# Scale and shift in halves of the features, and four projection chunks summed side by side by row blocks

## The reference

```python
    c_act = jax.nn.silu(c)
    mod = (c_act @ w_ada[l] + b_ada[l])[:, None, :]
    shift1, scale1, gate1, shift2, scale2, gate2 = jnp.split(mod, N_MOD, axis=-1)
    h = _rmsnorm(x, g_mix[l]) * (1.0 + scale1) + shift1
    proj = h @ w_in[l]
    a_u, a_v, b_q, b_k, b_v, c_q, c_k, c_v = jnp.split(proj, splits, axis=-1)
    # y_a: spatial gating, y_b: stick-breaking attention, y_c: dilated window attention with rope
    y = jnp.concatenate([y_a, y_b, y_c], axis=-1) @ w_out[l]
    x = x + (1.0 + gate1) * y
    ...   # a gated feed-forward with a short convolution, then an attention layer and a gated
    ...   # linear attention layer, each with a feed-forward, and a last norm
```

## Time and profile before

| | us |
|---|---|
| median of 3 runs | 939.43 |
| lowest, highest | 937.7, 939.97 |
| the profiled execution, its time | 938.27 |
| its span, first to last instruction | 936.5 |
| PE busy | 912.4 (97%) |
| DVE busy | 612.8 (65%) |
| ACT busy | 497.3 (53%) |

### The profile page before, as it was taken

How to read it: one execution, slowest core, us unless ns; L and a number is a source line. 1 busy time by engine, 2 the same in 40 slices (tenths; PEclk the granted TensorE clock), 3 DMA queues, 4 the chain that set the end, 5 groups by cost and what they waited for, 6 DMA issues and landing times.

```text
span 936.5 us, 17379 instructions
## 1 busy us (share of the span) xinstructions
PE 912.4 (97%) x7209; PEld 844.4 (90%) x7209; DVE 612.8 (65%) x970; ACT 497.3 (53%) x729; POOL 0.2 (0%) x4
## 2 busy tenths in 40 slices
PE   5899999999999999999999999999999999999997
PEld 2688788999999999878999999998999999988886
DVE  0665685786776775887765555576886765566664
ACT  3537774754555567665634434346656653344333
POOL 0000000000000000000000000000000000000000
PEclk9899999999999999999999999999999999999999
DMA  9998757676555578414365565555442655555541
GB/s 350 346 315 276 269 181 250 210 253 208 170 175 215 180 172 179 99 48 151 121 210 192 193 198 194 187 180 180 124 148 94 222 176 172 191 181 181 180 135 45
DMA packets 130698, 176.85 MB, mean 189 GB/s; under 512 B 19696, under 2 KB 108188, under 8 KB 130620
## 3 DMA queue, kind: packets, MB, share of 16 engines
q1 hardware_dynamic: 129852, 173.58, 56.8%
q10 hardware_dynamic: 768, 2.16, 0.7%
HBM read 174.68 MB, written 1.05 MB: 188 GB/s over the span
## 4 chain that ended last, share of the span: by engine, by line
PE 86%; DVE 6%; ACT 4%; DMA 2%; issue 2%; SPq 0%; ACTq 0%; DVEq 0%
PE psum L1591 25%; PE psum L1583 22%; PE psum L1584 21%; PE psum L1587 4%; PE psum L1588 4%; DMA raw<-in_w_ada_dram 2%; DVE w_lo L956 2%; PE psum L1685 1%; ACT w_hi L526 1%; PE psum L2190 1%; PE psum L2124 1%; PE psum L2145 1%; PE psum L2134 1%; DMA raw<-in_w_in_dram 1%; DVE h_lo L994 1%
## 5 line engine op out<-in xcount | busy, mean ns | idle before, releaser
L526 ACT ACTIVATE w_hi<-raw 128x2048 fp32r<-128x2048 f32 (+1 forms) x139 | 264.4, 1904 | 150.0 <-PE psum L1591 122.1
L1583 PE MATMUL psum<-h_hi,w_hi 128*128 128x256 f32 x1352 | 329.0, 283 | 1.5 <-DVE h_lo L1128 1.1
L956 DVE TENSOR_TENSOR w_lo<-raw,w_hi 128x2048 fp32r<-128x2048 f32 (+1 forms) x139 | 313.1, 2277 | 24.5 <-ACT w_hi L526 24.5
L1584 PE MATMUL psum<-h_lo,w_hi 128*128 128x256 f32 x1352 | 324.9, 280 | 0.0
L1583 PEld LDWEIGHTS psum<-h_hi,w_hi 128*128 128x128 f32 x1352 | 254.4, 188 | 11.0 <-issue 7.9
L1584 PEld LDWEIGHTS psum<-h_lo,w_hi 128*128 128x128 f32 x1352 | 255.0, 189 | 0.8
L1591 PE MATMUL psum<-h_hi,w_lo 128*128 128x256 f32 x1352 | 187.0, 280 | 0.7 <-DVE w_lo L956 0.5
L1591 PEld LDWEIGHTS psum<-h_hi,w_lo 128*128 128x128 f32 x1352 | 170.2, 188 | 1.5 <-DVE w_lo L956 1.3
L1324 DVE SCALAR_TENSOR_TENSOR arena<-psum,rstd 128x256 f32<-128x256 f32 x64 | 26.9, 424 | 132.0 <-PE psum L1591 130.1
L1583 PE MATMUL psum<-a_hi,w_hi 128*128 128x256 f32 x464 | 110.7, 280 | 0.6 <-DVE a_lo L1311 0.4
L1584 PE MATMUL psum<-a_lo,w_hi 128*128 128x256 f32 x464 | 110.3, 279 | 0.0
(11 more groups left out here) (274 smaller groups left out, 911.2 us busy)
## 6 DMA issues: line engine op xcount, KB each, us to landing
raw<-in_mlp_w_in_dram SPq DMA_DIRECT2D x32, 1024.0 KB, 5.6
raw<-in_mlp_w_out_dram SPq DMA_DIRECT2D x32, 1024.0 KB, 7.2
raw<-in_w_ada_dram SPq DMA_DIRECT2D x24, 1024.0 KB, 7.5
raw<-in_w_up_dram SPq DMA_DIRECT2D x22, 1024.0 KB, 5.1
raw<-in_gla_w_in_dram SPq DMA_DIRECT2D x12, 1024.0 KB, 5.3
raw<-in_w_down_dram SPq DMA_DIRECT2D x11, 1024.0 KB, 5.5
raw<-in_w_in_dram SPq DMA_DIRECT2D x10, 1024.0 KB, 8.1
raw<-in_w_out_dram SPq DMA_DIRECT2D x4, 1024.0 KB, 6.0
```

Source lines behind the costliest of these rows:

```text
L526: act.activation(halved(w_hi, m % SPLIT_SLOTS, SPLITS[m]), halved(raw, r % RAW_SLOTS, SPLITS[m]), ACT.Copy).then_inc(*mark("w_hi", m))
L956: dve.tensor_tensor(halved(w_lo, m % SPLIT_SLOTS, key), halved(raw, r % RAW_SLOTS, key), halved(w_hi, m % SPLIT_SLOTS, key).bitcast(F32), ...
L1583: pe.matmul(dst, high, both[0], start=start, stop=False, skip_group_check=True)
L1584: return pe.matmul(dst, high, both[1], start=False, stop=False, skip_group_check=True)
```

## The change

Scale and shift are both loaded and summed in halves of the features: pieces (1, 0), (1, 1), (0, 0), (0, 1) give scale and shift of feature tiles 0 to 3, and then two **row blocks** of `w_in` follow; a row block (`rows_in`) is 256 rows of the first four chunks, 1 MB in two DMAs. Then come the same six loads for tiles 4 to 7. The four chunks are summed side by side, two tiles in each of the banks 0 to 3: `rows_high` makes a block's 32 products with `w_hi`, `rows_low` its 16 with `w_lo`. Each half of scale and shift has its own turn (four transposes of 128 x 128), reduction and bias. `x` is turned first, with two of its four copies on DVE. The sums are copied out after the fourth block (`evict`). No `w_ada` pieces stand beside the first four chunks any more; the chunks 4 to 8 have two each. The six ropes and `w_sp` all stand behind in 4, `win_a` 0 to 3 behind in 5, and the turning of `rows` 2 to 4 and mod 2 behind in 6. The loads of constants move with them.

```diff
-ADA_BESIDE = [0, 1, 1, 2, 1, 1, 1, 1, 2, 1, 1]
+ADA_BESIDE = {4: 2, 5: 2, 6: 2, 7: 2, 8: 2, 9: 1, 10: 1}
+FIRST_CHUNKS = 4
...
-    s = [("ada", p, q) for p in (1, 0) for q in range(4)]
-    s.insert(5, ("in", 0))
-    for n in range(11):
-        s += [("in", n)] if n > 0 else []
-        s += [ada.pop(0) for _ in range(ADA_BESIDE[n])]
+    s = []
+    for half in range(2):
+        s += [("ada", p, 2 * half + j) for p in (1, 0) for j in range(2)] + [("rows_in", 2 * half + j) for j in range(2)]
+    for n in range(FIRST_CHUNKS, 11):
+        s += [("in", n)] + [ada.pop(0) for _ in range(ADA_BESIDE[n])]
...
-    extra = {0: [("angles",)], 1: [("rope", 0), ("rope", 1)], 2: [("rope", 2), ("rope", 3)], 3: [("rope", 4), ("rope", 5), ("w_sp",)],
-             4: [("win_a", 0), ("win_a", 1), ("rows", 2), ("rows", 3), ("rows", 4)],
-             5: [("win_a", 2)],
-             6: [("win_a", 3), ("stick_a", 0), ("stick_a", 1)],
+         ("round", 0), ("first", 0), ("round_low", 0), ("rows_high", 0), ("part", 1, 2), ("round", 1), ("round_low", 1),
+         ("rows_low", 0, 0), ("rows_low", 0, 1), ("part", 1, 3), ("angles",), ("rows_high", 1),
+         ("mod", 1, 1), ("gains", 0, 1), ("normed", 0, 1), ("part", 0, 2), ("part", 0, 3), ("rows_low", 1, 0), ("mod", 0, 1),
+         ("rows_low", 1, 1), ("round", 2), ("first", 1), ("round_low", 2), ("rows_high", 2), ("round", 3), ("round_low", 3),
+         ("rows_low", 2, 0), ("rows_low", 2, 1), ("rows_high", 3), ("round", 4), ("rows_low", 3, 0), ("rows_low", 3, 1),
+         ("evict", 0), ("evict", 1), ("round_low", 4), ("evict", 2), ("evict", 3)]
+    extra = {4: [("rope", t) for t in range(6)] + [("w_sp",)],
+             5: [("win_a", 0), ("win_a", 1), ("win_a", 2), ("win_a", 3)],
+             6: [("rows", 2), ("rows", 3), ("rows", 4), ("mod", 2), ("stick_a", 0), ("stick_a", 1)],
...
+                if kind == "rows_in":
+                    w = a["w_in"][0]
+                    return [(0, row_chunk(w[:, IN_COLS[0]:IN_COLS[0] + 3 * S], n * S)),
+                            (3 * S, row_chunk(w[:, IN_COLS[3]:IN_COLS[3] + S], n * S))], 2
...
+            def rows_high(q):
+
+                slot = weights(("rows_in", q))
...
+                for j in range(2):
+                    k = 2 * q + j
+                    operand(0, k)
+                    for n in range(FIRST_CHUNKS):
+                        for m in range(2):
+                            c = n * S + m * P
+                            high_by_both(first_sum(n, m), wview(w_hi, slot, 2)[:, j, c:c + P],
+                                         (h_hi[:, k, :], h_lo[:, k, :]), k == 0 and m == 0)
```

More of the change, by code:

```diff
@@ L45 @@
 CONST_W = {
-    "ident": P, "ones": P, "inv_freq": 1, "eps": 1, "one": 1, "ada_pick": 2, "ada_all": 1, "rope_swap": P, "tail": P, "tail_all": P, "before": P, "window": 3 * SP3, "upto": P,
+    "ident": P, "ones": P, "inv_freq": 1, "eps": 1, "one": 1, "rope_swap": P, "tail": P, "tail_all": P, "before": P, "window": 3 * SP3, "upto": P,
     "axial_swap": P, "axial_cos": S, "axial_sin": S, "head_mean": P,
@@ L305, in blocks3 @@
             return ap.rearrange("p (n c) -> p n c", c=P)
-        ring = {"n": 0, "last": {}, "set": range(len(IN_BANKS), ADA_BANK), "chunks": 0}
+        ring = {"n": 0, "last": {}, "set": range(FIRST_CHUNKS, ADA_BANK), "chunks": 0}
         def evacuated(*job):
@@ L659, in take_in @@
                     t = 2 * n + m
-                    if n < 3:
-                        copy(job, cqk[:, t, :], scale=0.125 if t < 3 else 1.0)
-                    elif n == IN_U:
+                    if n == IN_U:
                         act.wait_ge(*at("job", "w_sp", 0))
@@ L1038, in setup, with turn_x @@
                 columns(0)
+            def turn_x():
+                for j in range(1, 4, 2):
+                    dve.wait_ge(*at("job", "x", j))
+                    dve.tensor_copy(x_t[:, 2 * j:2 * j + 2, :], bank("x", j)[:, :].rearrange("p (k s) -> p k s", k=2))\
+                        .then_inc(*mark("dve_read", "x", j))
+                    for k in (2 * j, 2 * j + 1):
+                        same(("x_new", 0, k), ("dve_read", "x", j))
             def angles():
@@ new lines, in modulation @@
+            def modulation(p, half=None):
+                job = ("mod", p) if half is None else ("mod", p, half)
+                pe.wait_ge(*at("act_read", "ada", *job[1:]))
+                dst = take(pe, *job)
+                first = 0 if half is None else 512 * half
+                for b in range(4):
+                    ins = pe.transpose(dst[:, b * P:(b + 1) * P], ada[:, p % 2, first + b * P:first + (b + 1) * P], cst("ident"))
+                ins.then_inc(*mark("job", *job))
+            def rows_high(q):
+                slot = weights(("rows_in", q))
+                if q == 0:
+                    for n in range(FIRST_CHUNKS):
+                        ring["last"][n] = ("in", n, 1)
+                for j in range(2):
+                    k = 2 * q + j
+                    operand(0, k)
+                    for n in range(FIRST_CHUNKS):
+                        for m in range(2):
+                            c = n * S + m * P
+                            high_by_both(first_sum(n, m), wview(w_hi, slot, 2)[:, j, c:c + P],
+                                         (h_hi[:, k, :], h_lo[:, k, :]), k == 0 and m == 0)
@@ new lines, in rows_low @@
+            def rows_low(q, half):
+                key = ("rows_in", q)
+                slot = weights(key)
+                low_weights(key)
+                for n in (2 * half, 2 * half + 1):
+                    for j in range(2):
+                        for m in range(2):
+                            c = n * S + m * P
+                            ins = crossed(first_sum(n, m), wview(w_lo, slot, 2)[:, j, c:c + P], h_hi[:, 2 * q + j, :],
+                                          q == 3 and j == 1)
+                    if q == 3:
+                        ins.then_inc(*mark("job", "in", n, 1))
+                if half == 1:
+                    if q < 3:
+                        ins.then_inc(*mark("added", *key))
+                    else:
+                        ring["set"] = range(FIRST_CHUNKS - 1, ADA_BANK)
+                    used(key, ("added", *key) if q < 3 else ("job", "in", FIRST_CHUNKS - 1, 1))
```

150 lines of the change are left out of this document (58 added, 92 removed).

## The result

| | us |
|---|---|
| the changed kernel, median of four (three of them 946.89 to 948.32) | 947.90 |
| the kernel before, beside it, median (937.70 to 939.97) | 938.64 |
| ratio, 95% interval | 1.0089, 1.0072 to 1.0106 |
| the profiled execution of after, its span | 946.5 |

A forecast was written before the change was run, and what follows sets the result against it. A head waiting for loads, then PE alone, bounds the kernel. From 938.27 us: head -3.6, ropes +4.0, gate1 copy +2.8, sticks +1.0, gate2 +0.8, given back -1.0, clock +2.0, sum +6.0, give 944.3; range 937.3 to 949.

The forecast's parts named there:

- rival 3: Behind in 6: the clock falls a third time, up to 3.4 us more, 947.7; shares 0.12 with another rival.
- What bounds the kernel: Whole kernel: a head waiting for loads, then PE alone for 900 us; each new PE wait reaches the end.
- The head: Up to the third row block: start at 40.85, or 43.3 with 2.45 us of low clock; gains 3.6 us.
- The ropes: Behind in 4: PE runs out of banks at rope 4, since ACT splits in 5 late; new wait, +4.0 us.
- The copy of gate1: First piece of p = 3, behind in 6: PE waits for ACT's copy behind its split of in 7; +2.8 us.
- I take 3.5 between: In the gate1 copy: time between two load landings, chosen between 4.4 us in the trace and 2.8 by rate.
- The clock behind the ropes: After the rope wait: clock falls to 1.2 GHz for up to 6.9 us; +2.0 us, at most 3.4.
- The third low clock: After the wait at in 6: the clock may fall once more; left in the range, not in the sum.
- The sticks: Stick heads: ACT and DVE need 14.9 us from the gate1 copy, PE some 13.9; +1.0 us, bounds 0 and 2.
- gate2: Behind in 7: copy ends at +10.4 us, PE is there at +9.6; +0.8 us, bounds 0 and 1.7.

The follow-up runs named there:

- experiment 10: Experiment 6's kernel with the turning of rows 2 to 4 moved in front of the window scores behind in 5; 933.94 us, ratio 0.9952 to the kernel before.
- experiment 11: Experiment 10's kernel with 14 idle products of constants in front of the first row block; 932.02 us, ratio 0.9935 to the kernel before.
- experiment 5: The changed kernel with 14 idle products of constants on PE in front of the first row block; 943.97 us, one execution.
- experiment 1: The changed kernel with ACT's split of in 5 in front of its copies of in 4; 942.57 us, ratio 1.0034 to the kernel before.
- experiment 4: The changed kernel with idle products on PE in front of rope 4, rope 5 and `w_sp`; 945.83 us, one execution.
- experiment 2: The changed kernel with ACT's copies for gate1 and gate2 in front of its splits of in 7 and in 9; 945.97 us, ratio 1.0068.
- experiment 7: Experiment 6's kernel with the load of in 7 far ahead, rows 4 loaded earlier, mod 2 behind the stick steps of in 7; 942.00 us, ratio 1.0033.
- experiment 3: The changed kernel with the edits of experiment 1 and experiment 2 together; 942.25 us, ratio 1.0033 to the kernel before.
- experiment 6: The changed kernel with ACT's split of each chunk, in 5 to in 10, in front of its copies of the chunk before; 939.74 us, ratio 1.0007.
- experiment 8: Experiment 6's kernel with the turning of rows 2 to 4 moved behind the stick heads of in 7; 942.87 us, ratio 1.0037 to the kernel before.
- experiment 9: Experiment 8's kernel with 14 idle products of constants in front of the first row block; 941.59 us, ratio 1.0021 to the kernel before.

## Why the prediction was right, and where it wasn't

Forecast 944.3, range 937.3 to 949.0, measured 947.9: slower, as said, and inside the range, but 3.6 us above the forecast. The move was 9.3 where 6.0 was forecast, and the working gave less than 0.12 to the case that came (rival 3, a third low clock). Some of the agreement in the single terms is luck, as two of the points say, and 1.5 us of the profiled difference stand in a stretch that no term looked at. Point by point:

- **What bounds the kernel**: right. The head gained, every new wait reached the end, and from `gate_mix` to 450 us no wait moved the offset. Experiments 10 and 11 show the other side of it: without the waits the gain of the head is the gain of the kernel.
- **The head**: right within 0.7, in part by luck. First product at 23.50 (23.05 said), third row block at 42.66 (43.3 said). The term of the clock was mis-sized: 6.9 us at the low level were taken over from the kernel before, in the profile of after it was 3.4, and cost 1.3 instead of 2.45 (experiment 5); without the clock PE came some 0.5 us later than the working's 40.85. The size isn't fixed: the profile of experiment 10, with the same head, has 6.8 us there.
- **The ropes**: right in mechanism, size and place. In 5 starts 8.95 us behind the end of in 4 (8.6 said), PE was out of banks at rope 4, the fifth of the six, DVE L1179 ended the waits, and moving one split took most of it away (experiment 1).
- **The copy of gate1**: right in mechanism, too small by 1.6. The step that was mis-sized is "I take 3.5 between" the two landings: they were 82.1 and 86.5, 4.4 apart, the same as the 4.4 of the earlier trace rows, which I had as the upper bound. The first also took 5.6 and not 5.3 us. PE came 0.3 sooner than said, at +9.2. With 4.4 the working gives 3.7. The middle between a row of the same situation and a rate was a bad choice: the row was the better witness. The fabric ceiling named in the Trainium skill (DMA: Bandwidth & Descriptors, Specifications), 435 GB/s, would have given 2.4 between the landings, an estimate; the trace has 4.4, so it was even further off.
- **The clock behind the ropes**: came, 1.4 instead of 2.0 (experiments 1 and 4).
- **The third low clock**: it came, and I had left it in the range as rival 3 "up to 3.4 more, 947.7". It made PE's work up to the sticks 2.8 us longer. If a fall is forecast after a wait of 4.0 us, one after a second wait of 2.8 should have been given half a chance.
- **The sticks**: the number was right to 0.1, the two paths under it were not. From the start of the copy ACT and DVE took 16.2 us to the stick product (88.35 to 104.55) and not 14.9. PE came after 15.6 us, 2.8 of them from the low clock, so it would have needed 12.8 at full clock where "some 13.9" stands without a working. With these two the term is +3.4 and not +1.0, and the 2.8 of the clock lie inside it: +1.0 came out because the low clock filled the rest. Experiment 1 bears that out: half as much low time, the same 16.2 us (84.42 to 100.66), and 2.0 us of waiting instead of 0.6. What ACT's 14.9 left out is a landing: ACT stood 2.73 us for the load of in 8 (the row at 99.86 in the result). That load is issued when PE has consumed the second piece of p = 3 (92.69), and PE made those pieces for the most part at the low clock in both profiles; how much sooner it would have landed at full clock no run shows.
- **gate2**: right to 0.1. And without the wait for the copy in front of it a stick wait of 3.5 appeared (experiment 2): of two waits for one late split, the first takes most of the delay.
- **The landing of in 7**, which I took for the common cause after the first experiments, was not: experiment 7 had it early and the wait for DVE stayed. The prediction's account of the copy (a load, issued late, behind another) is right for after, since ACT did stand 10.62 us for that DMA. It isn't what must change: in experiment 10 the load lands at 83.6 and PE has no wait over 1 us behind the third row block.

## What stays open

The 1.5 us between 460 and 625 us. Set beside the kernel before, instruction for instruction, the offset of PE grows evenly there by 1.54 or 1.55 us in the profiled executions of after and of experiments 2, 3, 4, 6, 7, 8 and 9, and by nothing in those of 1, 5, 10 and 11. The granted clock is 1.00 in both kinds and no wait stands there. Each kernel has one profile, so I can't say whether it goes by the kernel or by the execution. It makes a single time or a single profile of this kernel uncertain by 1.5 us, and experiments 4 and 5 are read by their windows for that reason. The medians may hold it too, in one kernel and not in another, so a difference between two of them is sure only beyond that. The sign of the main results doesn't hang on it: at 450 us, in front of that stretch, the offset from the kernel before is +8.6 in after, -4.0 in 10 and -5.0 in 11. Nor was it tried what the third low clock costs by itself, with idle products in the wait of 4.33 us. Nor was the net worth of the idle products tried in the kernel before, which also had a low clock in its head.

## What to carry to other kernels

Work that is brought forward on one engine pays only if the in-order queues of the others allow it. For each wait that you take away, look for the next instruction that hangs on the same late event on another engine; here the order was ACT's copy, then DVE's copies of rows, then a bank held by stick heads, and of the arrangements tried only that of experiments 10 and 11 was free of all three. Here small helper steps (a copy of 0.5 us, a turn) did well in front of the operation that waits for a load, and badly in a ring of banks behind a holder that waits for another engine. Price a run of short waits twice, once for the time and once for the clock behind it; and where another engine's wait follows, ask how much of that second price it hides.
